# An opening modulation matrix taken in four column quarters instead of eight row tiles, and the order of the loads around it

## The reference, cut to what matters

```python
ada = (c @ w_ada + b_ada)[:, None, :]              # c: 1 x 1024, w_ada: 1024 x 6144
shift1, scale1, gate1, shift2, scale2, gate2 = jnp.split(ada, 6, axis=-1)
h = rmsnorm(x, g_norm1) * (1.0 + scale1) + shift1
proj = h @ w_in
(q_f, k_f, v_f, f_logit, q_d, k_d, v_d, q_i, k_i, w_i, gate_fox, gate_dsa) = jnp.split(proj, SPLIT_POINTS, axis=-1)
log_f = jax.nn.log_sigmoid((f_logit + b_forget).astype(jnp.float32))
iscore = ...            # from q_i, k_i, w_i: scores of an indexer
_, sel = lax.top_k(iscore, topk)                   # 64 keys for each query
```

## Time and profile before

| what | us |
|---|---|
| three runs, median (lowest to highest) | 1400.17 (1398.01 to 1400.55) |
| the profiled execution, its own time | 1399.87 |
| its span, first to last instruction | 1398.0 |
| PE busy of the span | 1342.0 (96%) |
| DVE busy | 824.5 (59%) |
| ACT busy | 660.9 (47%) |
| mean DMA rate over the span | 191 GB/s |

### The profile page before, as it was taken

How to read it: one execution, slowest core, us unless ns; L and a number is a source line. 1 busy time by engine, 2 the same in 40 slices (tenths; PEclk the granted TensorE clock), 3 DMA queues, 4 the chain that set the end, 5 groups by cost and what they waited for, 6 DMA issues and landing times.

```text
span 1398.0 us, 16261 instructions
## 1 busy us (share of the span) xinstructions
PE 1342.0 (96%) x6233; PEld 1099.2 (79%) x6233; DVE 824.5 (59%) x1118; ACT 660.9 (47%) x1052; POOL 82.3 (6%) x112
## 2 busy tenths in 40 slices
PE   2999999999999999999989999999999999999997
PEld 2777877788888788887767888888888888888885
DVE  5696756867565654457446653557553575855454
ACT  2656655454354543445655443445443444544442
POOL 3401100100000100001001000001000010100000
PEclk9999999999999999999999999999999999999999
DMA  9757654547445655555533655556556555565551
GB/s 336 247 197 255 227 195 151 181 181 287 164 181 177 214 182 199 192 181 181 181 121 120 212 190 200 181 181 224 182 197 195 181 190 184 189 201 194 179 189 59
DMA packets 156684, 268.37 MB, mean 192 GB/s; under 512 B 9445, under 2 KB 101685, under 8 KB 155584
## 3 DMA queue, kind: packets, MB, share of 16 engines
q1 hardware_dynamic: 148928, 239.45, 49.6%
q0 software_dynamic: 7680, 27.89, 5.9%
HBM read 266.21 MB, written 1.07 MB: 191 GB/s over the span
## 4 chain that ended last, share of the span: by engine, by line
PE 84%; DVE 7%; ACT 3%; DMA 3%; POOL 2%; issue 1%; SPq 0%; DVEq 0%; ACTq 0%; POOLq 0%
PE UP L666 16%; PE UP L668 15%; PE UP L667 15%; PE Y L666 10%; PE Y L668 10%; PE Y L667 10%; PE TB L738 4%; DVE WL L1361 2%; DMA X<-in_x 1%; POOL RS L598 1%; DMA RAW<-in_w_in 1%; POOL VAR L597 1%; ACT WH L1028 1%; DMA RAW<-in_ffn_w_gu 1%; PE Y L768 1%
## 5 line engine op out<-in xcount | busy, mean ns | idle before, releaser
L1361 DVE TENSOR_TENSOR WL<-RAW,WH 128x1024 fp32r<-128x1024 f32 (+2 forms) x446 | 512.4, 1194 | 181.8 <-ACT WH L1028 175.7
L1028 ACT CAST WH<-RAW 128x1024 fp32r<-128x1024 f32 (+2 forms) x446 | 434.2, 1031 | 218.4 <-PE Y L668 135.0
L666 PE MATMUL UP<-WH,AH 128*128 128x512 f32 (+1 forms) x1104 | 445.2, 403 | 6.5 <-DVE WL L1361 4.3
L668 PE MATMUL UP<-WH,AL 128*128 128x512 f32 (+1 forms) x1104 | 431.0, 390 | 0.0
L667 PE MATMUL UP<-WL,AH 128*128 128x512 f32 (+1 forms) x1104 | 429.8, 389 | 0.0
L666 PEld LDWEIGHTS UP<-WH,AH 128*128 128x128 f32 x1104 | 208.0, 188 | 52.4 <-issue 10.9
L668 PEld LDWEIGHTS UP<-WH,AL 128*128 128x128 f32 x1104 | 207.6, 188 | 44.0
L667 PEld LDWEIGHTS UP<-WL,AH 128*128 128x128 f32 x1104 | 208.4, 189 | 39.4 <-issue 0.7
L666 PE MATMUL Y<-WH,HH 128*128 128x512 f32 (+1 forms) x496 | 193.6, 390 | 0.0
L668 PE MATMUL Y<-WH,HL 128*128 128x512 f32 (+1 forms) x496 | 191.6, 386 | 0.0
L667 PE MATMUL Y<-WL,HH 128*128 128x512 f32 (+1 forms) x496 | 191.5, 386 | 0.0
(11 more groups left out here) (209 smaller groups left out, 934.3 us busy)
## 6 DMA issues: line engine op xcount, KB each, us to landing
RAW<-in_ffn_w_gu SPq DMA_DIRECT2D x176, 512.0 KB, 4.9
RAW<-in_ffn_w_down SPq DMA_DIRECT2D x80, 512.0 KB, 4.2
RAW<-in_w_mlp SPq DMA_DIRECT2D x64, 512.0 KB, 4.3
RAW<-in_w_in SPq DMA_DIRECT2D x38, 512.0 KB, 5.2
PIECE<-in_w_ada POOLq DMA_DIRECT2D x32, 512.0 KB, 5.4
RAW<-in_a_w_in SPq DMA_DIRECT2D x24, 512.0 KB, 4.7
WADA<-in_w_ada SPq DMA_DIRECT2D x7, 1024.0 KB, 10.0
RAW<-in_w_out SPq DMA_DIRECT2D x8, 512.0 KB, 3.8
```

The lines of the kernel that those rows point to most:

```text
L666: pe.matmul(dst, ah, wh, start=first, stop=False)
L668: return pe.matmul(dst, al, wh, start=False, stop=last)
L1028: act.copy(WH[:, u % 2, q * n:(q + 1) * n], raw_half(u, q // 2)[:, (q % 2) * n:(q % 2 + 1) * n]).then_inc(wh_done, 1)
L1361: ve.tensor_tensor(WL[:, u % 2, o], raw_half(u, q // 2)[:, (q % 2) * n:(q % 2 + 1) * n], WH[:, u % 2, o].bitcast(F32), ALU.subtract).then_ ...
```

## The change

The first 2048 columns of w_ada are taken in four column quarters. Quarter q holds columns 256q to 256q+255 of shift1 and of scale1, so k tiles 2q and 2q+1 of the activations. The buffer WADA keeps its size and holds two quarters; a quarter comes by eight DMAs of 256 KB with rows of 1 KB (before: seven of 1 MB with rows of 8 KB and two of 512 KB). SP may load quarters 2 and 3 when `ada_done` says 1 and 2. The load of x moves to the middle of quarter 0, that of unit 0 to behind quarter 0, that of unit 1 behind quarter 3.

Of each quarter's eight row tiles ACT multiplies tile 0 (`opening_product`), DVE adds tiles 1 to 6 (`accumulate`, twelve instructions of 256 columns), and PE adds tile 7 by fp32 matmuls straight against c (`ada_columns`, four matmuls of one column, and four for the sum over partitions). `scales` makes SHIFT and SCALE of two k tiles. ACT now makes MOD too for quarters 0 to 2. PE takes unit 0 by quarters, both token tiles for each k (`first_unit`), into other PSUM banks, and runs matmuls whose result is not used in between (`keep_busy`: 10, 6, 6, 12, 12, 8). The forget gates of both token tiles are done in one set of three ACT instructions, and wait no longer between the two token tiles of unit 1. Both indexer turns come after tok 0 of unit 1. `MODULATION` moves the two pieces of unit 0 to unit 1 and unit 3. The diff, cut to its core:

```diff
-MODULATION = (2, 0, 1, 1, 3, 3, 3, 3, 3, 3, 2)
+MODULATION = (0, 1, 1, 2, 3, 3, 3, 3, 3, 3, 2)
@@ sync
-            for k in range(4):
-                sp.dma_start(WADA[:, k, :], wada[:, k, 0:2 * D]).then_inc(in_wada[k], 16)
-            sp.dma_start(X[:, :, :], ...).then_inc(in_x, 16)
-            for k in range(4, KT):
-                sp.wait_ge(wada_used, k - 3)
...
+            ada_pair(0, 0)
+            ada_pair(0, 1)
+            sp.dma_start(X[:, :, :], ...).then_inc(in_x, 16)
+            ada_pair(0, 2)
+            ada_pair(0, 3)
+            load(0)
+            for q in range(1, 4):
+                if q >= 2:
+                    sp.wait_ge(ada_done, q - 1)
+                for m in range(4):
+                    ada_pair(q, m)
+            for u in range(1, len(UNITS)):
...
+                load(u)
@@ gpsimd
-            gp.wait_ge(ada_done, 2)
+            gp.wait_ge(ada_done, 4)
@@ tensor
+            def keep_busy(n, unused):
+                for _ in range(n):
+                    pe.matmul(unused[:, 0:REV], IDR[:, :], CMR[:, :], start=True, stop=True)
+            def ada_columns(q):
+                pairs = [(a, i) for a in range(2) for i in range(2)]
+                pe.wait_ge(*wada_landed(q, KT - 1))
+                for a, i in pairs:
+                    pe.matmul(sum_column(q, a, i), wada_row(q, KT - 1, a)[:, i * P:(i + 1) * P], CC[:, KT - 1:KT],
+                              start=True, stop=False)
+                pe.wait_ge(acc_done, 12 * (q + 1))
+                for a, i in pairs:
+                    o = a * 256 + i * P
+                    mm = pe.matmul(sum_column(q, a, i), ACC[q][:, o:o + P], ONES[:, 0:1], start=False, stop=True)
+                mm.then_inc(ada_done, 1)
+            def first_unit(q):
+                for k in (2 * q, 2 * q + 1):
+                    pe.wait_ge(mod_low, k + 1)
+                    quarters(0, 0, (k + 1) * width)
+                    for tok in range(TOK):
+                        mm = three(FIRST[tok][:, 0:width], AH[:, k, ts], AL[:, k, ts], WH[:, 0, w], WL[:, 0, w],
+                                   k == 0, k == KT - 1)
...
+            keep_busy(10, FIRST[1])
+            pe.wait_ge(in_small, 48)
             rev_row(0)
+            ada_columns(0)
             for tok in range(TOK):
                 pe.wait_ge(xhat_done, tok + 1)
                 chain_turns("h", tok, Z)
+                keep_busy(6, FIRST[1])
+            first_unit(0)
+            for q in range(1, 4):
+                ada_columns(q)
+                keep_busy(12 if q < 3 else 8, TB[0])
+                first_unit(q)
@@ scalar
+            xhat(0)
+            round_unit(0, (0,))
+            xhat(1)
+            round_unit(0, (1,))
+            opening_product(1)
+            turned(0)
+            round_unit(0, (2,))
+            turned(1)
+            round_unit(0, (3,))
+            mod_highs(0, True)
+            opening_product(2)
+            mod_highs(1, True)
+            opening_product(3)
+            mod_highs(2, True)
+            mod_highs(3, False)
+            round_unit(1, (0, 1))
@@ vector
+            accumulate(0, range(1, 7))
             split_unit(0, (0,))
+            scales(0)
+            split_unit(0, (1, 2, 3))
+            accumulate(1, range(1, 5))
+            mod_low_of(0)
+            mod_low_of(1)
+            accumulate(1, range(5, 7))
+            for q in (2, 3):
+                accumulate(q, range(1, 3))
+                scales(q - 1)
+                accumulate(q, range(3, 5))
+                mod_low_of(2 * q - 2)
+                mod_low_of(2 * q - 1)
+                accumulate(q, range(5, 7))
```

More of the change, by code:

```diff
@@ L306, in build @@
         XT = PIECE[:, :, :].rearrange("p a b -> p (a b)").rearrange("p (k n) -> p k n", n=256)
+        ACC = [ADA[:, q, 0:HALF] for q in range(4)]
         MOD = ROWS[:, :, :].rearrange("p a b -> p (a b)").rearrange("p (k n) -> p k n", n=256)
@@ L686, in wide @@
                 for k in range(kts):
-                    if u == 0 and tok == 0:
-                        pe.wait_ge(mod_low, k + 1)
                     if chain and k % 4 == 0:
@@ L826, in _ @@
                 chain_turns("h", tok, Z)
-            for h in range(2):
-                pe.wait_ge(*((acc_half, 1), (wada_used, KT))[h])
-                for a in range(2):
-                    for k in range(4 * h, 4 * h + 4):
-                        mm = pe.matmul(Y[0][h][:, 4 * a + k % 4:4 * a + k % 4 + 1], ADA[:, a, k * P:(k + 1) * P],
-                                       ONES[:, 0:1], start=True, stop=True)
-                mm.then_inc(ada_done, 1)
+                keep_busy(6, FIRST[1])
[4 more added lines that the diff above has]
+                first_unit(q)
             att = 0
-            late = []
+            late = [(("qi", tok), 3) for tok in range(TOK)]
             head = None
-            for u in range(11):
+            for u in range(1, 11):
                 name = UNITS[u][0]
@@ L1201, in _ @@
                     if tok == 0 and before == "misc":
-                        index_in(1)
+                        round_unit(2, (2, 3))
+                        for n in range(TOK):
+                            index_in(n)
                     elif tok == 0 and before in ("qf", "kf"):
@@ L1503, in mod_lows, with accumulate @@
-            def mod_lows(first, end):
-                for k in range(first, end):
-                    ve.wait_ge(mod_done, k + 1)
-                    ve.wait_ge(mod_high, k + 1)
-                    ve.tensor_tensor(AL[:, k, :], MOD[:, k, :], AH[:, k, :].bitcast(F32), ALU.subtract
-                                     ).then_inc(mod_low, 1)
-            split_unit(0, (0,))
+            def accumulate(q, ks):
+                for k in ks:
+                    ve.wait_ge(*wada_landed(q, k))
+                    for a in range(2):
+                        if k == 1:
+                            ve.wait_ge(first_done, q + 1)
+                        else:
+                            ve.wait_ge(acc_done, 12 * q + 2 * (k - 2) + a + 1)
+                        dst = ACC[q][:, a * 256:(a + 1) * 256]
+                        ve.scalar_tensor_tensor(dst, wada_row(q, k, a), CC[:, k:k + 1], dst, ALU.mult, ALU.add
+                                                ).then_inc(acc_done, 1)
@@ new lines, in scales, with mod_whole @@
+            def scales(q):
+                ve.wait_ge(ada_done, q + 1)
+                for i in range(2):
+                    k = 2 * q + i
+                    ve.tensor_scalar(SHIFT[:, k:k + 1], sum_column(q, 0, i), COLS[:, k:k + 1], None, ALU.add)
+                    ins = ve.tensor_scalar(SCALE[:, k:k + 1], sum_column(q, 1, i), COLS[:, 8 + k:9 + k],
+                                           COLS[:, 16 + k:17 + k], ALU.add, ALU.mult)
+                ins.then_inc(scale_done, 1)
+            def mod_whole(k):
+                ve.tensor_scalar(MOD[:, k, :], XT[:, k, :], SCALE[:, k:k + 1], SHIFT[:, k:k + 1],
+                                 ALU.mult, ALU.add).then_inc(mod_done, 1)
```

222 lines of the change are left out of this document (106 added, 116 removed).

## The result

The changed kernel takes 1416.74 us (median of 4 runs, 1412.84 to 1419.27) against 1400.09 us for the kernel before (4 runs); the ratio is 1.012, 95% interval 1.0103 to 1.0137. It is slower by 16.7 us, where the prediction had 3.3 and a range up to 1408.0. The profiled execution is the fastest of the four: 1412.84, with a span of 1411.1 us, 13.1 longer than before's.

A forecast was written before the change was run, and what follows sets the result against it. PE's own work was taken as the bound (busy 96%), with DVE having nothing to spare from unit 2's start to 104.5 us. 0.4 + 2.6 + 0.3 = 3.3 us on 1399.87 gives 1403.2, 1403.4 on the median; range 1398.5 to 1408.

The forecast's parts named there:

- The two pieces: Two w_ada pieces moved into DVE's stretch without slack: first row maxima 2.6 us later, PE's probabilities wait 0.33 becomes 2.9.
- The 0.3 added for a piece that lands late: Piece in front of the first row maxima, its load let go later: 0.3 us added, between 0 and 1.1.
- The clock behind that wait: Low-clock rival, chance 0.12: PE's 2.9 us wait at the probabilities may drop the clock, costing 1.7 us; alone 1405.
- To K: Opening up to PE's start of unit 2 (kd): forecast at 64.9 us, 0.4 later than before.
- the half: Load of unit 2's second half, issued by SP at 53, fully meeting POOL's pieces and table: there at 60.3 us.
- To unit 1: Opening up to PE's start of unit 1 (qd): 48.8 us against 47.32, 1.5 us later.
- The sums: Column sums of quarters 1, 2 and 3 in the opening: ready at 32.5, 38.7 and 44.9 us.
- The round: One quarter's turn in the opening, from one `ada_done` to the next: 6.2 us, as long as its load (6.1).
- The wait for the forget gates: Unit 1's second token tile on PE no longer waits for the forget gates: 1.4 us gone.
- Small loads: Rival, chance 0.08: 256 KB loads run at 240 GB/s, a quarter takes 8.7 us instead of 6.1; 1406.
- The faster rival: Rival, chance 0.10: loads set the opening's pace, rounds about 5.3 us or less, unit 0 over at 42; 1396.6.

## Why the prediction was wrong, step by step

**The two pieces: right.** 2.9 was forecast for the wait, 2.97 measured, and 2.97 again with the pieces moved alone. The 0.3 added for a piece that lands late did not come: DVE sits idle nowhere between 79 and 118 us. That DVE has no slack between K and 104 us was the right reading of the earlier trace rows.

**The clock behind that wait: a rival, and it was the case.** It stood at 1.7 us with a chance of 0.12, worked out from the 214 us stretch. Every wait of 2.9 to 3.0 us in these runs was followed by a stretch at half clock, of 3.4 us in four cases and 6.8 in six; the 6.8 us of the changed kernel cost 3.15. Put as a rival, it should have been a term of the sum, though the one stretch of the earlier trace rows could not tell that it comes each time.

**To K: the step that failed.** K was forecast at 64.9 and came at 73.79. The text had seen that the half would meet POOL's transfers "fully" and took 60.3, by the 7.4 us of the kernel before. There they had gone out 3.4 to 4.5 us ahead of the half, here 1.2 and 0.1 us: 11.2 us, ACT on the half at 66.73.

```profile
54.41 1.10 POOL L641 DMA_DIRECT2D PIECE<-in_w_ada  x2
55.51 0.93 POOL L614 DMA_DIRECT2D TAB<-rev_rows  x1
...
55.56 0.88 SPq L544 DMA_DIRECT2D RAW<-in_w_in  x2
...
66.73 1.99 ACT L1083 CAST WH<-RAW 128x1024 fp32r<-128x1024 f32 x2 [8.21 <-DMA RAW<-in_w_in]
```

The 8.9 us add up from 2.6 of later issue (unit 1 itself is late), 3.8 longer on the way, and 2.5 more from ACT's round to K (7.1 for 4.6; the same way took 5.6 in the earlier trace rows, so 1 us was missing from the text's sum, and 1.65 are the half clock). Against the kernel before, PE's wait of 4.95 more is the 3.8 on the way and some 1.3 that unit 1 ends earlier after the half's issue (8.1 us instead of 9.4), since its wait for the forget gates is gone. The prediction carried a duration of the earlier trace rows over to another meeting: what counts is all that stands in the engines' queues with the half, 3.7 MB in the 10 us from 57 on, at 372 GB/s (unit 3's first half, issued at 59.34 behind it, is part of that).

The trace shows how the half fared (packets, MB, share of the 16 engines' time; q0 is POOL's queue, q1 SP's). From 55.5 to 59 us, with the half issued at 55.56, and then from 61 to 64 us:

```profile
q0 software_dynamic: 251, 0.96, 85.1%
```

```profile
q0 software_dynamic: 182, 0.74, 67.3%
q1 hardware_dynamic: 188, 0.36, 36.4%
```

SP's queue moved nothing for the first 3.4 us, and then as many packets as POOL's, but of 1.9 KB each against 4.1, so a third of the bytes.

**To unit 1: mis-sized, +4.45 for +1.5.** The steps came as told: x at 11.55 (10.6), DVE's quarter 1 behind the fourth split at 25.20 (24.5), PE's first matmul at 28.84 (28.3). (The text's own loads, 3.3 + 1.5 + 3.0 + 2.5, put x at 10.3, not 10.6.)

```profile
24.44 0.85 DVE L1442 TENSOR_TENSOR WL<-RAW,WH 128x664 fp32r<-128x664 f32 x1 [0.77 <-ACT WH L1083]
25.20 3.25 DVE L1565 SCALAR_TENSOR_TENSOR ADA<-WADA,COLS,ADA 128x256 f32<-128x256 f32 x8
28.37 0.76 DVE L1587 TENSOR_TENSOR AL<-ROWS,AH 128x256 fp32r<-128x256 f32 x2
```

The sums came at 33.95, 40.47 and 47.45 instead of 32.5, 38.7 and 44.9. The first of these was missed within the text's own terms: from 28.3 on, twelve matmuls 0.28 apart and eight one-column products of 0.21 end at 33.3, not 32.5. The round was put at 6.2, with PE's share counted in part; as a chain it is twelve matmuls 1.9, eight one-column products 1.75, scales 0.7, ACT's four 2.1, AL 0.4: 6.85, and 6.5 and 7.0 were measured. DVE's wait of 0.5 for quarter 3, whose issue waits for the second sum, comes on top.

**The wait for the forget gates: right.** 1.8 us went from unit 1's two tiles, and the run with the other banks alone shows that by itself it only moves to the half.

**Small loads: right to set aside.** The 256 KB loads came at 348 GB/s (345 forecast). The faster rival failed at what it named: rounds of 6.5 to 7, not 5.3. No run changes the size of the loads alone.

## What to carry to other kernels

Before moving a load, list what else is issued in the microseconds around its new place, on which queue and in packets of what size: here a 1 MB load took 11.2 us to be usable instead of 7.4. A wait that a change adds to TensorE costs itself and, after each of the ten of 2.9 to 3.0 us here, a stretch at the low clock that cost 3.15 us in the one case worked out; put that into the sum. And a gain ahead of an engine without slack (here DVE behind K) is kept by that engine, so find the next bound first.
